# Twelve steps of the last product with seven block products in place of eight

## The reference

```python
        h = rmsnorm_2(x, g_ffn[l])
        u = causal_dwconv(h @ w_up[l], ffn_conv_w[l]) + ffn_conv_b[l]
        gate, val = jnp.split(u, 2, axis=-1)
        x = x + (jax.nn.silu(gate) * val) @ w_down[l]
    return rmsnorm_2(x, g_final)
```

## Time and profile before

| | |
|---|---|
| median of 3 runs | 2432.59 us (2432.27 to 2432.82) |
| the profiled execution, its time | 2432.91 us |
| its span, first to last instruction | 2431.0 us |
| TensorE busy | 2421.2 us, 10738 matmuls |
| VectorE busy | 1487.4 us (61%) |
| ScalarE busy | 1267.9 us (52%) |
| DMA, mean over the span | 225 GB/s |
| mean granted TensorE clock | 0.999 |

### The profile page before, as it was taken

The page is one execution under the profiler, slowest core; times in us unless marked ns, Lnnn a source line. Parts: engine busy times, 40 slices in busy tenths (PEclk is TensorE's granted clock), DMA queues, the critical chain, the costliest instruction groups (busy, mean ns, idle before and its releaser), DMA issues.

```text
span 2431.0 us, 27750 instructions
## 1 busy us (share of the span) xinstructions
PE 2421.2 (100%) x10738; PEld 2008.2 (83%) x10738; DVE 1487.4 (61%) x1877; ACT 1267.9 (52%) x1580; POOL 189.4 (8%) x349
## 2 busy tenths in 40 slices
PE   9999999999999999999999999999999999999998
PEld 8888888888888888888888888888888888888887
DVE  7575555667555555555555865786577776666444
ACT  7555566445444444444444654454566666665443
POOL 0000000001000000000000110110111110110000
PEclk9999999999999999999999999999999999999999
DMA  8777655778667667676667776887788878787564
GB/s 274 226 224 225 195 197 176 227 230 253 220 212 226 210 222 217 211 228 211 210 214 235 245 242 210 256 247 233 240 242 249 244 239 244 241 241 231 191 193 154
DMA packets 155012, 545.85 MB, mean 225 GB/s; under 512 B 20096, under 2 KB 20608, under 8 KB 154624
## 3 DMA queue, kind: packets, MB, share of 16 engines
q1 hardware_dynamic: 131120, 470.91, 60.5%
q0 software_dynamic: 23184, 72.37, 10.9%
q10 hardware_dynamic: 576, 0.79, 0.1%
HBM read 505.72 MB, written 38.27 MB: 224 GB/s over the span
## 4 chain that ended last, share of the span: by engine, by line
PE 99%; DMA 0%; ACT 0%; DVE 0%; issue 0%; DVEq 0%
PE ps L1540 99%; DMA XG<-in_x 0%; PE ps L1638 0%; PE ps L1658 0%; PE ps L1659 0%; PE ps L1639 0%; PE ps L1684 0%; PE ps L1671 0%; PE ps L1685 0%; PE ps L1672 0%; PE ps L1628 0%; PE ps L1627 0%; PE ps L1629 0%; PE ps L1626 0%; ACT tmp L1036 0%; ACT X L1045 0%
## 5 line engine op out<-in xcount | busy, mean ns | idle before, releaser
L1082 DVE TENSOR_TENSOR wl<-raw,wh 128x1024 fp32r<-128x1024 f32 x874 | 1067.9, 1223 | 917.7 <-ACT wh L765 916.7
L765 ACT CAST wh<-raw 128x1024 fp32r<-128x1024 f32 x874 | 915.3, 1049 | 1057.4 <-PE ps L1540 1041.9
L1540 PE MATMUL ps<-wh,x1g_hi 128*128 128x512 f32 x704 | 273.9, 389 | 0.0
L1540 PE MATMUL ps<-wl,x1g_hi 128*128 128x512 f32 x704 | 273.9, 389 | 0.0
L1540 PE MATMUL ps<-wh,x1g_lo 128*128 128x512 f32 x704 | 273.9, 389 | 0.0
L1540 PE MATMUL ps<-wh,act_hi 128*128 128x512 f32 x704 | 273.9, 389 | 0.0
L1540 PE MATMUL ps<-wl,act_hi 128*128 128x512 f32 x704 | 273.9, 389 | 0.0
L1540 PE MATMUL ps<-wh,x4g_hi 128*128 128x512 f32 x704 | 273.9, 389 | 0.0
L1540 PE MATMUL ps<-wl,x4g_hi 128*128 128x512 f32 x704 | 273.9, 389 | 0.0
L1540 PE MATMUL ps<-wh,x4g_lo 128*128 128x512 f32 x704 | 273.9, 389 | 0.0
L1540 PE MATMUL ps<-wh,act_lo 128*128 128x512 f32 x704 | 273.9, 389 | 0.0
(11 more groups left out here) (308 smaller groups left out, 3131.8 us busy)
## 6 DMA issues: line engine op xcount, KB each, us to landing
raw<-in_w_in SPq DMA_DIRECT2D x196, 512.0 KB, 4.3
raw<-in_w_ffn_in SPq DMA_DIRECT2D x176, 512.0 KB, 4.2
raw<-in_w_up SPq DMA_DIRECT2D x176, 512.0 KB, 4.5
raw<-in_w_ffn_out SPq DMA_DIRECT2D x88, 512.0 KB, 4.2
raw<-in_w_down SPq DMA_DIRECT2D x88, 512.0 KB, 4.3
rows<-Y POOLq DMA_DIRECT2D x67, 512.0 KB, 4.7
Z<-rows POOLq DMA_DIRECT2D x268, 128.0 KB, 4.9
raw<-in_w_o SPq DMA_DIRECT2D x32, 512.0 KB, 4.7
```

Source lines behind the costliest of these rows:

```text
L765: e.copy(wh[:, i % RING, :], raw[:, slot, :]).then_inc(rounded, 1)
L1082: e.tensor_tensor(wl[:, r, :], raw[:, i % RAW, :], wh[:, r, :].bitcast(F32), ALU.subtract).then_inc(remainder, 1)
L1540: return e.matmul(dst, weights, x, start=start, stop=stop, skip_group_check=True)
```

## The change

The last product is done in two pairs of chunks (columns 0 to 1023, then 1024 to 2047). In a pair the granules of the two chunks for the same K tiles follow each other, so that one step holds two K tiles by two chunks. Seen as a product of 2 x 2 blocks (two halves of positions by two K tiles, times two K tiles by two chunks), a step takes eight block products of three matmuls each, 24 matmuls. In 12 of the 44 steps (six K pairs, in each pair of chunks) seven block products of sums of blocks take their place, 21 matmuls. Such a step is a **unit** below; i is its first granule.

- The sums of activations (`xs_sum`, `xs_hi`, `xs_lo`) are made once for the six K pairs, in three rounds, from step 5 of the last product on. They lie where the operand of the up product was (`o_a`).
- For a unit ScalarE and VectorE split three weight blocks as they are (`base_hi`, `base_lo`, 128 x 1536, in buffers of their own) and VectorE makes four sums of weight blocks in `tmp` (`sums`), which are split into the ring's slots of granules i and i + 1 (`forms_hi`, `forms_lo`, 128 x 2048). The raw slots are freed by `sums` instead of by the subtraction.
- TensorE does the unit in two parts: `multiply_base` (9 matmuls) at step i + 4, `multiply_forms` (12) behind the matmuls of granule i + 3. In both pairs a plain step stands between two units; the first unit of the first pair is granule 18 and the last 38, those of the second pair 54 and 74 of 88.
- Three of the seven products and a fourth that two chunks share go to four banks of their own. After the last unit of a pair they are copied to `tmp` (`shared_out`) and added to X in six operations (`shared_sums` to `shared_second`).
- The final gains lie in another place (`o_y`) and are fetched at step 20. The weights in HBM are arranged for the new order of blocks.

The core of the diff (what follows the new numbering only, and the new semaphore counts, is left out):

```diff
+SEVEN = (8, 10, 12, 14, 16, 18)
+DOWN_ORDERS = ((0, 1, 2, 3, 4, 5, 6, 7, 9, 8, 11, 10, 13, 12, 15, 14, 17, 16, 19, 18, 20, 21),
+               (0, 1, 2, 3, 4, 8, 5, 10, 6, 12, 7, 14, 9, 16, 11, 18, 13, 15, 17, 19, 20, 21))
+DOWN_TAILS = (20, 16)
...
+        def product_side_by_side(src, operand, q, bank, order, tail, keys, afters, late, cleared):
+            pair = Pair([], 4 - bank)
+            for n, key in enumerate(keys):
+                chunk = named[key] = Chunk("N", bank + 2 * n, None)
+                chunk.cleared = cleared[n]
+                pair.chunks.append(chunk)
+            rows = list(order[:tail])
+            for u, p in enumerate(rows):
+                if p in SEVEN:
+                    former = list(seven.values())[-1] if seven else None
+                    unit = Seven(len(granules), p, pair, former, SEVEN.index(p))
+                    pair.units.append(unit)
+                    seven[unit.i] = unit
+                for n in range(2):
+                    granules.append((pair.chunks[n], src[2 * q + n, p], operand, 2 * p, u == 0, False))
+            for k, name in enumerate(("shared_out", "shared_sums", "shared_first", "shared_last", "shared_second")):
+                later(pair.units[-1].i + 7 + k, lambda name=name: do(name, q))
+            for n in range(2):
+                for p in order[tail:]:
+                    granules.append((pair.chunks[n], src[2 * q + n, p], operand, 2 * p, False, p == order[-1]))
+                chunk = pair.chunks[n]
+                chunk.last = len(granules) - 1
+                later(chunk.last + RING + late, lambda s=chunk.last + RING + late, n=n: afters[n](s, pair.chunks[n]))
+            return pair
...
-        later(len(granules) + RING, lambda: do("load_gf"))
-        for n in range(4):
-            product(t["w_down"], "N", "act2", PAIRS44, ("down", n), plan_down(n), n)
+        down_from = len(granules)
+        later(down_from + 20, lambda: do("load_gf"))
+        for j in range(3):
+            later(down_from + 5 + 4 * j, lambda j=j: do("xs_sum", j))
+            later(down_from + 6 + 4 * j, lambda j=j: do("xs_hi", j))
+            later(down_from + 7 + 4 * j, lambda j=j: do("xs_lo", j))
+        down_pairs = []
+        for q in range(2):
+            cleared = ([("pool_out", 1)], [("x_split", 1, 1)]) if q == 0 else ([("shared_out", 0)], [("shared_out", 0)])
+            down_pairs.append(product_side_by_side(
+                t["w_down"], "act2", q, (4, 0)[q], DOWN_ORDERS[q], DOWN_TAILS[q], [("down", 2 * q), ("down", 2 * q + 1)],
+                [plan_down(2 * q), plan_down(2 * q + 1)], (5, 0)[q], cleared))
...
+            elif s in seven or s - 1 in seven:
+                if s - 1 in seven:
+                    do("base_hi", s - 1)
+                    do("base_lo", s - 1)
+                    do("sums", s - 1)
...
+                if s - 3 in seven:
+                    do("forms_hi", s - 3)
+                    do("forms_lo", s - 3)
...
-            if 0 <= i < total - RING:
+            if i - 1 in seven:
+                do("multiply_base", i - 1)
+            elif 0 <= i < total - RING and i not in seven:
                 do("multiply", i)
+                if i - 3 in seven:
+                    do("multiply_forms", i - 3)
...
+        def used_at(i):
+            return multiplied, multiply_count[("multiply_forms", i - i % 2) if i - i % 2 in seven else ("multiply", i)]
...
+                if i - RAW in seven:
+                    e.wait_ge(*at("sums", i - RAW, 0))
+                elif i - RAW - 1 in seven:
+                    e.wait_ge(*at("sums", i - RAW - 1, 1))
+                else:
+                    e.wait_ge(remainder, rounded_at(i - RAW))
...
+                elif name == "base_hi":
+                    i, = args
+                    former = seven[i].former
+                    e.wait_ge(landed[i % RAW], 16 * (i // RAW + 1))
+                    e.wait_ge(landed[(i + 1) % RAW], 16 * ((i + 1) // RAW + 1))
+                    if former is None:
+                        e.wait_ge(*at("xs_lo", 2))
+                    else:
+                        e.wait_ge(multiplied, multiply_count["multiply_base", former.i])
+                    e.copy(base_hi.rearrange("p k c -> p (k c)"), two_slots(raw, i)[:, 512:2048]).then_inc(done[name], 1)
+                elif name == "forms_hi":
+                    i, = args
+                    e.wait_ge(*used_at(i - RING))
+                    e.wait_ge(*used_at(i - RING + 1))
+                    e.wait_ge(*at("sums", i, 1))
+                    e.copy(two_slots(wh, i), tile_sums.rearrange("p k c -> p (k c)")).then_inc(done[name], 1)
+                elif name == "xs_hi":
+                    j, = args
+                    e.wait_ge(*at("xs_sum", j))
+                    e.copy(seven_tiles(operands["act2"][0], j)[:, :, 1], xs_out[:, :, 0])
+                    e.copy(xs_hi[:, 2 * j:2 * j + 2], xs_out[:, :, 1:4]).then_inc(done[name], 1)
+                elif name == "shared_out":
+                    q, = args
+                    pair = down_pairs[q]
+                    e.wait_ge(*at("forms_lo", pair.units[-1].i))
+                    e.wait_ge(multiplied, multiply_count["multiply_forms", pair.units[-1].i])
+                    for k in range(4):
+                        e.copy(tile_sums[:, k, :], ps[:, pair.shared + k, :]).then_inc(done[name], 1)
...
+                elif name == "base_lo":
+                    i, = args
+                    e.wait_ge(*at("base_hi", i))
+                    e.tensor_tensor(base_lo.rearrange("p k c -> p (k c)"), two_slots(raw, i)[:, 512:2048],
+                                    base_hi.rearrange("p k c -> p (k c)").bitcast(F32), ALU.subtract).then_inc(done[name], 1)
+                elif name == "sums":
+                    i, = args
+                    unit = seven[i]
+                    b12, b11, b22, b21 = (two_slots(raw, i)[:, 512 * k:512 * k + 512] for k in range(4))
+                    if unit is not unit.pair.units[0]:
+                        e.wait_ge(*at("forms_lo", unit.former.i))
+                    elif unit.former is None:
+                        e.wait_ge(*at("act2_lo", 21))
+                    else:
+                        e.wait_ge(*at("squares", "out", 1))
+                    e.tensor_tensor(tile_sums[:, 0:2, :], two_slots(raw, i)[:, 512:1536].rearrange("p (k c) -> p k c", k=2),
+                                    b12.unsqueeze(1).broadcast_to([P, 2, 512]), ALU.add).then_inc(done[name], 1)
+                    e.wait_ge(*at("sums", i, 0))
+                    e.tensor_tensor(tile_sums[:, 2, :], tile_sums[:, 0, :], b22, ALU.add).then_inc(vector_step, 1)
+                    e.wait_ge(vector_step, next(step))
+                    e.tensor_tensor(tile_sums[:, 3, :], tile_sums[:, 2, :], b21, ALU.add).then_inc(done[name], 1)
+                elif name == "forms_lo":
+                    i, = args
+                    e.wait_ge(*at("forms_hi", i))
+                    e.tensor_tensor(two_slots(wl, i), tile_sums.rearrange("p k c -> p (k c)"), two_slots(wh, i).bitcast(F32),
+                                    ALU.subtract).then_inc(done[name], 1)
...
+                elif name == "xs_sum":
+                    j, = args
+                    hi, lo = (seven_tiles(x, j) for x in operands["act2"])
+                    if j == 0:
+                        e.wait_ge(*through(last_up))
+                    else:
+                        e.wait_ge(*at("xs_lo", j - 1))
+                    e.wait_ge(*at("act2_lo", SEVEN[2 * j + 1]))
+                    e.tensor_tensor(xs_in[:], hi.bitcast(F32), lo.bitcast(F32), ALU.add).then_inc(vector_step, 1)
+                    e.wait_ge(vector_step, next(step))
+                    e.tensor_tensor(xs_out[:, :, 0:2], xs_in[:, :, 1:2].broadcast_to([P, 2, 2, P]), xs_in[:, :, 0:4:3],
+                                    ALU.subtract).then_inc(vector_step, 1)
+                    e.wait_ge(vector_step, next(step))
+                    e.tensor_tensor(xs_out[:, :, 2], xs_in[:, :, 0], xs_out[:, :, 1], ALU.subtract).then_inc(vector_step, 1)
+                    e.wait_ge(vector_step, next(step))
+                    e.tensor_tensor(xs_out[:, :, 3], xs_in[:, :, 2], xs_out[:, :, 2], ALU.subtract).then_inc(done[name], 1)
+                elif name == "xs_lo":
+                    j, = args
+                    e.wait_ge(*at("xs_hi", j))
+                    hi, lo = (seven_tiles(x, j)[:, :, 1] for x in operands["act2"])
+                    e.tensor_tensor(lo, xs_out[:, :, 0], hi.bitcast(F32), ALU.subtract)
+                    e.tensor_tensor(xs_lo[:, 2 * j:2 * j + 2], xs_out[:, :, 1:4], xs_hi[:, 2 * j:2 * j + 2].bitcast(F32),
...
+            def three(dst, x, w, start, stop):
+                (x_hi, x_lo), (w_hi, w_lo) = x, w
+                matmul(dst, x_hi, w_hi, start, False)
+                matmul(dst, x_hi, w_lo, False, False)
+                return matmul(dst, x_lo, w_hi, False, stop)
...
```

(58 more changed lines are left out.)

75 lines of the change are left out of this document (60 added, 15 removed).

## The result

| | median of 18 runs, us | lowest to highest |
|---|---|---|
| before | 2432.53 | 2431.84 to 2433.33 |
| changed | 2437.14 | 2434.80 to 2438.84 |

The ratio is 1.0018, with an interval of 1.0011 to 1.0025: 4.6 us were lost where 0.4 had been forecast as a gain. The spread grew too, from 1.5 us to 4.0. The profiled execution of the changed kernel took 2436.24 us, its span is 2434.4 us.

A forecast was written before the change was run, and what follows sets the result against it. TensorE, busy for the whole span, was taken to bound the kernel. The terms -8.16 + 5.1 + 1.4 + 1.05 + 0.2 summed to -0.4 us, forecasting 2432.2 us, range 2429.2 to 2438.0 us.

The forecast's parts named there:

- What goes: Last product, TensorE: twelve units remove 36 matmuls at 0.2267 us each, -8.16 us.
- Gap behind the last unit: Behind each pair's last unit, granule i+4 waits for its ring slot: TensorE idle 2.54 us, twice, 5.1 us.
- rival 3: TensorE's clock falls in a 2.5 us gap: 2.2 us lost, twice, 2436.6 us; chance 8%.
- Before the first unit: At granule 20, VectorE's subtractions, tap chains, activation sums and waits for ScalarE make it late once: 1.4 us.
- Each further unit: First pair's later units: cycle through the weight load takes 10.41 us against TensorE's 10.20; 0.21 late five times, 1.05 us.
- the forecast's 5.91: Later units' load cycle without the landing: base cast, remainder, sums and small steps, 5.91 us.
- rival 2: Load cycle is worse: landing of 5.3 us, late by 1.0 each time, 2438.0 us; chance 10%.
- Second pair and final gains: Second pair's lateness hidden by 3.1 us spare; moved load of final gains delays granule 24, taken as 0.2 us.

The follow-up runs named there:

- eighth run: The seventh run's kernel with K pair 8 plain and first in the first pair, eleven units for twelve: 2425.62 us, ratio 0.9972.
- second run: Changed kernel with the granule behind each pair's last unit split into the base blocks' buffers instead of the ring slot: 2429.01 us, ratio 0.9986.
- fifth run: Kernel before with ten long TensorE idles added in the last product, the cast waiting for the granule just ahead: 2474.83 us, ratio 1.0175.
- the first: Changed kernel with eleven matmuls of a zero tile behind the last unit of each pair: 2434.27 us, ratio 1.0007.
- third run: Changed kernel with the first unit of the first pair done as two plain granules: 2434.86 us, ratio 1.0010.
- fourth run: Changed kernel with loads of the five later units of the first pair fetching only 64 of 1024 columns: 2433.37 us, ratio 1.0006.
- the seventh: Second run's kernel with VectorE's steps in a unit reordered, first sums before the base remainder, each raw slot released once read: 2426.74 us, ratio 0.9977.
- sixth run: Kernel before with ten short TensorE idles in the last product, only the subtraction waiting for the matmuls ahead: 2449.49 us, ratio 1.0069.

## Why the prediction was wrong

By its own steps:

- **What goes, -8.16 us.** Right. The last product without its excess is 8.15 shorter, and the eighth run keeps this rate to 0.1 us.
- **Gap behind the last unit, 2.54 twice.** The cause and the size of the idle were right: 2.61 us measured twice, ended by VectorE's subtraction, and gone with the slot (second run). **This is the step that failed**, since it priced the gap by its idle alone. A gap of this length can also lower the clock: 3.40 us for the two here, 1.57 each by the fifth run. The forecast had this apart as rival 3, at 8%. Its mechanism is what happened; its price, 2.2 each, was somewhat high, because the low level lasts 3.41 us here, and not the 4.5 read from the kernel's start.
- **Why rival 3 got 8%.** "Against: here it held longer than the gap" rested on one stretch, the 4 us from the last matmul until the clock was seen lower. The same end of the kernel shows how little one sample binds. In the changed kernel:

```profile
2426.30:2428.70 2.40, 0.27 (x2) 0.00 (x0) 0.90 (x3) 0.92 (x3) 0.00 (x0) 1.00 0.79 295
2428.90:2431.00 2.10, 0.00 (x0) 0.00 (x0) 1.58 (x5) 1.33 (x2) 0.00 (x0) 0.50 0.10 37
```

  Here it fell 2.6 us behind the start of the last matmul (2426.18), before 4.2, and over all ten profiles between 2.4 and 5.2 (2.7 in the second run, 5.2 in the first). So one hold of 4 us said nothing against a fall in a gap of 2.5. It fell behind ten of ten in the fifth run, two of two here, and one of two each in the third and fourth.
- **Before the first unit, 1.4.** 1.63 measured, ended by VectorE's subtraction. That VectorE is short of time there stands by the third run, where the idle goes with the unit. Its chains, its sums and its waits were not separated.
- **Each further unit, 1.05.** 1.78, in unequal parts and not five times 0.21. That the cycle runs through the load is shown by the fourth run and, from the other side, by the seventh. The cycle was right and the landing was mis-sized. The load that closes it is the second of the two for the next unit, issued when `sums` frees its slot. For units 26, 30, 34 and 38 it was issued at 2243.90, 2254.53, 2265.51 and 2275.99 and landed 4.7, 5.0, 4.5 and 4.7 us later, where I took 4.5. The base casts of these units start 10.63, 10.98, 10.48 and 10.98 us behind the one before; less TensorE's 10.20 that is 0.43, 0.78, 0.28 and 0.78, and TensorE lost 0.05, 0.73, 0.25 and 0.75. Unit 22, whose load took 3.9, lost nothing. So the forecast's 5.91 holds to 0.05 in three of the four; in the last there are 0.3 more that I can't place. The forecast's own condition for rival 2 (from 4.6 on) was met by three of these four; its price was taken at a landing of 5.3, which none of them reached. Over all 22 loads of this stretch the median is 4.9 (below: KB each, median us from issue to landing). The Trainium skill (page DMA: Bandwidth & Descriptors, section Anatomy of one DMA) gives an estimate of 3.2 us for such a load by its fixed part and its rate; the trace does not agree where loads are this close (4.5 to 5.0 for those that close the cycle).

```profile
raw<-in_w_down SPq DMA_DIRECT2D x22, 512.0 KB, 4.9
GF<-in_gfin SPq DMA_DIRECT2D x1, 1024.0 KB, 7.2
```

- **Second pair and final gains.** The spare time covered the second pair but for 0.2 us. The load of the gains landed after 7.2 us, less than the 8.2 that I feared for it; no idle at its place stands out of the unequal ones around it, so whether its 0.2 is in them stays open.

The sum again, with the measured sizes: -8.15 + 5.22 + 3.40 + 1.63 + 1.78 + 0.20 + 0.26 = +4.34 us for -0.4 forecast. Of the 4.7 between them the clock is 3.4; the gaps, granule 20, the later units and the spread over all others together were 1.3 longer than taken. Each rival had one thing go wrong on top of the forecast's rest; here the clock fell and the small idles were longer, too.

What stays open: the changed kernel's own spread of 4.0 us. Executions with one or two low stretches (1.7 us each) account for a part of it at most: those with a mean clock of 0.998 alone lie between 2434.80 and 2438.84 us, and the three with 0.997 at 2436.24, 2437.35 and 2438.02. And why one gap of two was spared in the third and fourth run is not shown; the spared ones are as long as the others, 2.61 us, so at this length it isn't the length that decides.

## What to carry to other kernels

A gap in TensorE, where that engine is otherwise never idle, has two prices: its length, and what the clock does behind it. So read the granted clock behind every idle of a trace, more than one, before you price a gap that the change creates; one long hold is no bound. Where work is removed from the bounding engine, look first for buffers that the new order frees too late: here one slot and one order of VectorE's steps made a change that lost 4.6 us into one that gains 6.9.

## What the runs showed of the hardware

- Behind 2.6 to 2.7 us without a matmul the clock went from 1.00 to 0.50 in 14 of 16 cases (ten of them the evenly spaced ones of the fifth run), each time for 3.41 us, after which matmuls of 512 columns went from 0.43 back to 0.23 us apart, with TensorE busy in between. Behind idles of 1.5 to 1.9 us it never did (ten in the sixth run, and those at the first unit in five profiles). At times it fell only when matmuls had resumed (behind the second pair of the changed kernel: last start 2394.64, next 2397.48, low from 2398.1), so the idle that brought it down stands ahead of the place where it is seen. The Trainium skill (page TensorE: Matmul & The Clock Gate, section What's actually happening) says that an idle array goes back to half its rate and that activity releases it; behind the 2.6 us idles these runs agree in 14 cases of 16.
- Even at a clock of 1.00 the first matmul behind an idle takes longer to its successor: 0.34 us for 0.23 (2257.46 to 2257.80).
